# A diffusion step on one core: decay products issued a step ahead, prompt experts shared between two engines, and an earlier last slot

## The reference

```python
for l in range(DEPTH):                                   # 2 layers
    yp, ... = trunk_layer(yp, cond_ctx, lp, None, None)  # prompt
    ys, _   = trunk_layer(ys, cond_lat, lp, rope, ...)   # sample, reads the context caches

def trunk_layer(x, cond, lp, rope, ctx):
    m = silu(cond) @ lp['w_ada'] + lp['b_ada']
    sh1, sc1, g1, sh2, sc2, g2 = jnp.split(m, 6, axis=-1)
    mix, ctx_out = mixer(rmsnorm(x, n1) * (1 + sc1) + sh1, ...)
    x = x + g1 * mix
    x = x + g2 * peer_ffn(rmsnorm(x, n2) * (1 + sc2) + sh2, ...)

# mixer: x @ w_in -> attention | SSD scan, forward and backward | conv module -> concat @ w_out
# SSD of one chunk of 128 tokens and one direction, 8 heads:
lmat   = jnp.exp(segsum(a))                              # decays between tokens
scores = jnp.einsum('bclhn,bcshn->bhcls', ch, bh) * lmat
y_diag = jnp.einsum('bhcls,bcshp->bclhp', scores, xdt)
y_off  = ch . state . exp(a_cum)                         # then the state is updated

# peer_ffn, per block of 128 tokens: 8 heads choose 16 experts each, so 128 slots
s   = einsum(h @ w_q, sub_keys);  idx, gate = two-level top-16 of s
act = gelu(einsum('thkd,td->thk', u_tab[idx], hb))
out = einsum('thk,thkd->td', gate * act, v_tab[idx])
```

## Time and profile before

| | us |
|---|---|
| median of 3 runs | 4883.53 (4875.92 to 4887.87) |
| the profiled execution's own time | 4890.8 |
| its span in the trace | 4888.7 |
| PE / DVE / ACT / POOL busy | 3740.6 / 3316.4 / 876.5 / 1708.5 |
| granted TensorE clock, mean | 0.917 of full |

### The profile page before, as it was taken

How to read it: one execution, slowest core, us unless ns; L and a number is a source line. 1 busy time by engine, 2 the same in 40 slices (tenths; PEclk the granted TensorE clock), 3 DMA queues, 4 the chain that set the end, 5 groups by cost and what they waited for, 6 DMA issues and landing times.

```text
span 4888.7 us, 35992 instructions
## 1 busy us (share of the span) xinstructions
PE 3740.6 (77%) x10702; PEld 1857.5 (38%) x10702; DVE 3316.4 (68%) x8175; ACT 876.5 (18%) x2387; POOL 1708.5 (35%) x1374
## 2 busy tenths in 40 slices
PE   7578677858777778788878786785977787777776
PEld 6463434623232223235535443344432332322222
DVE  1546766666887868754574866666678887786666
ACT  0111125441101010010121111353310100100101
POOL 0001121573444435422222011217544454444432
PEclk9788788979999999999989897887999999999999
DMA  8335346775999999999969353557489999999998
GB/s 267 104 118 181 140 181 211 263 250 202 407 420 409 420 419 413 421 374 392 358 245 349 106 205 132 199 197 275 172 335 417 415 415 421 414 421 421 401 421 342
DMA packets 342147, 1497.68 MB, mean 306 GB/s; under 512 B 31424, under 2 KB 176448, under 8 KB 178112
## 3 DMA queue, kind: packets, MB, share of 16 engines
q0 software_dynamic: 184320, 1342.26, 68.8%
q1 hardware_dynamic: 157632, 153.13, 9.8%
HBM read 1491.97 MB, written 3.31 MB: 306 GB/s over the span
## 4 chain that ended last, share of the span: by engine, by line
PE 31%; DMA 30%; DVE 24%; POOL 5%; issue 5%; ACT 4%; SPq 1%; DVEq 0%; POOLq 0%; ACTq 0%
DMA uv_ring<-uv,expert_index 23%; PE expert_acc L766 13%; DVE uv_ring L1341 5%; DMA arena<-uv,expert_index 5%; PE rotating L997 4%; POOL arena L696 3%; PE rotating L795 3%; PE rotating L829 2%; DVE diag L1350 2%; POOL uv_ring L718 2%; DVE arena L1341 2%; DVE arena L1498 1%; DMA w_ring<-w_ada 1%; DVE arena L1711 1%; PE rotating L746 1%
## 5 line engine op out<-in xcount | busy, mean ns | idle before, releaser
L766 PE MATMUL expert_acc<-uv_ring,diag 128*128 128x512 f32 x3408 | 1723.8, 638 | 420.2 <-DVE diag L1350 410.2
L718 POOL DMA_INDIRECT uv_ring<-uv,expert_index x940 | 1103.3, 1174 | 2546.3 <-PE expert_acc L766 1994.4
L766 PEld LDWEIGHTS expert_acc<-uv_ring,diag 128*128 128x128 f32 x3408 | 626.8, 199 | 1407.5 <-DVE diag L1350 870.3
L1341 DVE CUSTOM_DVE_ANT_0 uv_ring<-uv_ring,arena 128x1024 f32<-128x1024 f32 x684 | 836.9, 1224 | 233.5 <-DMA uv_ring<-uv,expert_index 230.6
L766 PE MATMUL expert_acc<-arena,diag 128*128 128x512 f32 x1360 | 681.7, 628 | 179.4 <-DVE diag L1350 147.5
L1055 ACT ACTIVATE gelu<-u_dot 128x1 f32<-128x1 f32 x1280 | 260.2, 204 | 2868.8 <-DVE u_dot L1341 2868.1
L1350 DVE TENSOR_SCALAR diag<-const_mats,expert_gate,gelu 128x128 f32<-128x128 f32 x1192 | 437.2, 367 | 280.3 <-ACT gelu L1055 193.0
L718 POOL DMA_INDIRECT arena<-uv,expert_index x340 | 392.2, 1153 | 453.4 <-PE expert_acc L766 436.5
L1341 DVE CUSTOM_DVE_ANT_0 uv_ring<-uv_ring,prompt_rows 128x1024 f32<-128x1024 f32 x256 | 403.3, 1579 | 191.7 <-DMA uv_ring<-uv,expert_index 148.3
L1341 DVE CUSTOM_DVE_ANT_0 arena<-arena 128x1024 f32<-128x1024 f32 x340 | 416.1, 1224 | 92.9 <-DMA arena<-uv,expert_index 91.2
L766 PEld LDWEIGHTS expert_acc<-arena,diag 128*128 128x128 f32 x1360 | 240.3, 194 | 601.6 <-DVE diag L1350 380.6
(11 more groups left out here) (208 smaller groups left out, 3098.9 us busy)
## 6 DMA issues: line engine op xcount, KB each, us to landing
w_ring<-w_ada SPq DMA_DIRECT2D x66, 512.0 KB
w_ring<-w_in SPq DMA_DIRECT2D x64, 512.0 KB
w_ring<-w_pq SPq DMA_DIRECT2D x64, 512.0 KB
w_ring<-w_out SPq DMA_DIRECT2D x32, 512.0 KB
uv_ring<-w_ada SPq DMA_DIRECT2D x30, 512.0 KB, 5.5
uv_ring<-uv,expert_index POOLq DMA_INDIRECT x940
arena<-b_ada SPq DMA_DIRECT2D x48, 128.0 KB
arena<-uv,expert_index POOLq DMA_INDIRECT x340, 15.1
```

The costliest lines, as they stand in the source:

```text
L718: pool.indirect_dma_start(out=UV[j], out_offset=None, in_=uv, in_offset=bass.IndirectOffsetOnAxis(ap=idxs[:, n % 2, k:k + 1], axis=0)).the ...
L766: ins = pe.matmul(acc[:, half, :], diag[:, TURN[m] % DIAGS, :], UV[SLOT_AT[m]][:, D + 512 * half:D + 512 * half + 512], start=(k == 0), st ...
L1341: V_.tensor_tensor_reduce(UV[j][:, 0:D], UV[j][:, 0:D], rows_of(n), 1.0, 0.0, ALU.mult, ALU.add, dots[:, m % DOTS:m % DOTS + 1]).then_inc( ...
```

## The change

Three things are edited.

1. In the SSD loop TensorE issues the two dd products of step i+1 between yo and y of step i; only those of step 0 stand ahead of the loop. `psum_order` follows. On ACT the three gelus of a step's advances move behind the exponentials of the next step.
2. Among the prompt's slots, `by_pool` gave POOL all from 84 to 127 (44 of a layer). Now POOL has the odd ones from 84 to 107 and all from 108 on (32); the 12 even ones from 84 to 106 go to TensorE.
3. The table has 5 advances at n2 and 4 at pq tile 7, 145 in all. Slot 127, the fold and `add_peer` now stand at pq tile 7.

```diff
-                       ("head", range(24), 1), ("wo", range(0, 16, 2), 2), ("wo", range(1, 16, 2), 1), ("n2", [7], 3), ("pq", range(8), 2))
+                       ("head", range(24), 1), ("wo", range(0, 16, 2), 2), ("wo", range(1, 16, 2), 1), ("n2", [7], 5), ("pq", range(7), 2), ("pq", [7], 4))
...
-POOL_FROM = 84
+POOL_FROM, POOL_ALL = 84, 108
...
-    return n % NBLK == 0 and k >= POOL_FROM
+    return n % NBLK == 0 and (k >= POOL_FROM and k % 2 == 1 or k >= POOL_ALL)
...
-                    for i, (d, b) in enumerate(ssd_steps(g)):
+                    def decays(i):
+
                         pe.wait_ge(*s_arow.at(l, g, i))
                         for k in range(2):
                             t = fill("dd", l, g, 2 * i + k)
-                            done(pe.matmul(t, C[:, C_US if d else C_LS, :], Em[i % 2][:, 4 * k:4 * k + 4, :],
+                            done(pe.matmul(t, C[:, C_US if ssd_steps(g)[i][0] else C_LS, :], Em[i % 2][:, 4 * k:4 * k + 4, :],
                                            start=True, stop=True), "dd")
+
+                    decays(0)
+                    for i, (d, b) in enumerate(ssd_steps(g)):
...
                         done(pe.matmul(t, BC[:, 1, b * P:(b + 1) * P], Sbd[:, d, :], start=True, stop=True), "yo")
+                        if i + 1 < 2 * nb:
+                            decays(i + 1)
                         pe.wait_ge(*s_xdt.at(l, g, i))
...
                                                  ACT.Exp).then_inc(free["dd"].sem, 1)
-                        beside.point("st", i)
+                        if i:
+                            beside.point("st", i - 1)
+                    beside.point("st", 2 * nb - 1)
```

More of the change, by code:

```diff
@@ L289, in psum_order @@
             out += [("cT", l, g, b) for b in range(nb)]
+            out += [("dd", l, g, 0), ("dd", l, g, 1)]
             for i in range(2 * nb):
-                out += [("dd", l, g, 2 * i), ("dd", l, g, 2 * i + 1), ("yo", l, g, i), ("y", l, g, i), ("st", l, g, i)]
+                out.append(("yo", l, g, i))
+                if i + 1 < 2 * nb:
+                    out += [("dd", l, g, 2 * i + 2), ("dd", l, g, 2 * i + 3)]
+                out += [("y", l, g, i), ("st", l, g, i)]
             out += [("yT", l, g, b) for b in range(nb)]
```

## The result

The changed kernel takes 4820.18 us (median of 4 runs, 4817.62 to 4825.25) beside 4885.7 us for the kernel before, run on the same chip (4 runs, 4875.92 to 4891.81): a ratio of 0.9869, 95% interval 0.985 to 0.9888. It is about 65 us faster. The profiled execution's span went from 4888.7 to 4819.6 us.

What follows compares the result with a forecast made beforehand. No engine being full in SSD, it read chains: DVE's there, POOL's cycle in the output stage, POOL then TensorE in the query projection. SSD -46, output stage -6, query projection +21.6 gave -30, from 4883.5 to 4853 us; range 4825 to 4886.

Steps and rivals of the forecast that it cites:

- Exponential waits, -41.8: SSD: DVE's waits for exponentials go except in step 0; 20.0 us saved per sample, 3.83 in layer 1's prompt, 2 lost in layer 0's.
- The clock adds to it ... I take 4 in all, between 0 and 9: SSD samples: without the 2.7 us gap before y, y runs more often at TensorE's upper clock; 4 us saved in all.
- a wait at the upper clock is about 1.09: SSD: DVE's shortest wait for y, from the longest wait 2.4 less the 1.32 between two y rows; 2.8 us a sample.
- Output stage, -6: Output stage: POOL no longer longest, TensorE's tiles and sums plus waits set the time; 3 us saved a layer, 6 in all.
- The four waits: Output stage: TensorE waits for late-built diagonals at tiles 2, 6, 10 and 14, 3 us each, 12 together.
- Query projection, +21.6: Query projection: fold delays the second half 20.0 us, tail shrinks 9.2; net 10.8 us lost a layer, 21.6 in all.
- hold: Query projection: the fold, ahead of the transposes, waits for POOL's last add; second half starts 20.0 us later a layer.
- tail: End of query projection to the sample's first dot: 14.9 us before, forecast to get 9.2 us shorter a layer.
- The wait did not move to y: Rival, SSD: dd at the lower clock delays y, 46 saved becomes about 17; net 0, 4883 us; chance 0.13.
- TensorE's clock did not fall in the output stage: Rival, output stage: four waits drop TensorE's clock; at 0.70 the stage takes 126 us, total 4911; chance 0.09 for slower.
- rival of more from SSD and the output stage: SSD and output stage: every y at the upper clock (9 us), 8 a layer in output stage; 4840 us; chance 0.14.
- rival without a hold: Query projection: fold finds POOL done, so 18 us saved there; -70 in all, 4813 us; chance 0.10.

## Why the prediction missed

**Exponential waits, -41.8: right for the samples and layer 1's prompt.** 20.0 us a sample and 3.8 in that prompt went, as worked out. Layer 0's prompt lost 1.7 us of the 2 taken, but only 0.3 of them by the mechanism named, the pair ahead of the first y. The rest was the clock behind a gap of 3.73 us, so the near number is luck.

**"The clock adds to it ... I take 4 in all, between 0 and 9": this is the step that failed.** The same term measured 26 us in the samples' waits (y 5.5 + 7.4, st 6.7 + 6.8) and 3.9 more in layer 1's prompt, less the 1.4 lost in layer 0's. That is some 25 of the 35 us by which the forecast fell short. Two things were wrong in it. I took the y of 2.33 us for one at the upper clock, "a wait at the upper clock is about 1.09"; it was already touched by the fall, and the real values are 1.97 and 0.73. The 1.97 stood in my own rows: it is the first row, the same 16 matmul records, there behind a gap of 0.83 us. And I priced only y, though the text said that DVE stands three times in each step: st stands right behind y, took 2.02 us against 1.08 in 13 of the 16 steps, and its 8 us a sample were a row of the same view as the earlier trace rows. The mechanism was named and the direction right; the term was over six times too small, and its upper bound, built from y alone, too low as well. The two experiments on the gap, one filling it in the old order and one opening it in the new, show it from both sides.

The Trainium skill, "TensorE: Matmul & The Clock Gate", section "Why this matters for your kernels", says that idle gaps between bursts put the clock back to half. The traces agree that the clock falls around such gaps, but not that each gap brings it to half for the product behind it: of the 14 y products behind a gap of 2.96 us, four took 3.65 us and three 1.97. The prediction took the rule for every y as 10.6 us a sample and set it aside; y's part was 5.5 and 7.4 us, so that was right for y. With st's part, which it did not price, it is 12.2 us in layer 0 and 14.2 in layer 1.

**Output stage, -6: near, in part by luck.** 9.1 us were measured up to the first query tile, but 3.1 us of each layer's 4.6 and 4.5 lie in the norm behind the stage, which the sum did not have. From the first tile to the end of the last dot it is 98.8 us against 100.3, so 1.5 saved a layer, half of the 3 taken. The four waits are there, at 2.4 to 2.6 us instead of 3, with four small ones beside them: 11.7 us in all, for the 12 taken. The granted clock was 0.95, not 0.92. Left out were the drain of the last tile and the dot behind it, 2.0 us.

**Query projection, +21.6: right.** +17.8 measured, hold 36.4 of 40, tail -18.6 of -18.4. TensorE stood 23.13 us before the fold ("some 24"), and 5.8 us lie between the end of the last query matmul and the sample's first dot (1142.0 to 1147.76). The forecast had "about 6" and called it the time from the last score, though its sum counts from the last query matmul.

**The rivals.** None decided. The wait did not move to y, POOL was not done at the fold, and TensorE's clock did not fall in the output stage (0.95). The rival of more from SSD and the output stage, 0.14, has the right place but was sized by the same wrong bound, 9 us for the clock. The time of 4820 lies nearest to the 4813 of the rival without a hold, which the trace rules out: TensorE stood 23.13 us before the fold.

## What to carry to other kernels

When a gap ahead of a matmul is removed, price every product behind it up to the engine's next stand at both clocks, and take the upper-clock duration from a stretch whose granted clock is 1.00, not from a row of a stretch at 0.85. To test whether a gap costs clock, fill it with a repeat of the product before it: if the kernel gets faster by added work, the gap did cost. An item that waits for a slow engine belongs late in a queue, where its input has long arrived: the same fold cost 17 to 19 us a layer ahead of the transposes and under 2 us four tiles into the second half.

## What the runs showed of the hardware

At a gap of 3.08 us y itself could still run in 1.97 us, and only st and the sums behind it were slow (1.70, and 3.00 where 1.88 is usual); gaps of 1.76 us in each step left the granted clock at 1.00 in six steps in a row. One of them:

```profile
632.50:645.30 12.80, 10.87 (x36) 5.41 (x37) 11.72 (x23) 4.25 (x8) 4.34 (x3) 1.00 0.69 245
```

So the fall can show in the matmuls behind the one that ended the gap, and not in that one.

One small operation of DVE's in the norm took 2.94 us in the kernel before (2.93 in layer 1), where its like take 0.17, while POOL ran a gather and an add of 2.35 us; with the split, without adds there, it takes 0.17:

```profile
1010.90 2.35 POOL L696 TENSOR_TENSOR arena<-uv_ring,arena 128x1024 f32<-128x1024 f32 x1
1013.52 0.95 POOL L718 DMA_INDIRECT uv_ring<-uv,expert_index  x1 [0.27 <-POOL arena L696]
1014.49 2.35 POOL L696 TENSOR_TENSOR arena<-uv_ring,arena 128x1024 f32<-128x1024 f32 x1
```

```profile
1013.94 2.94 DVE L1314 TENSOR_SCALAR newton<-newton 128x4 f32<-128x4 f32 x1
```

The operation ends with the add, at 1016.9; this is most of the 3.1 us that the norm got shorter with the split. The Trainium skill, "SBUF — State Buffer", section "SBUF: two separate sides", has DVE and GpSimd share a pair of ports: a DVE operation in a two-port mode, or with two inputs in SBUF, and one of GpSimd's lock each other out for a whole instruction. The common end is in keeping with it. But the trace does not show the mode of this one-input operation, its row begins 0.55 us before the add's, and no run here varied the two alone, so the cause is not shown.

POOL's gathers show something like it, and they are part of its pace of 4.30 us a slot. Between 906 and 1115 us of the kernel before, 35 gathers were issued while DVE ran a dot, and they took 1.3 to 1.8 us; the seven others took 0.95. In the changed kernel, 880 to 1085 us, it was 12 of 15 beside a dot, and none of the 26 others. The gather of the earlier trace rows, 1.65 us from 940.81 on, stands beside this dot, which itself took 3.29 us instead of 1.22:

```profile
938.34 3.29 DVE L1341 CUSTOM_DVE_ANT_0 uv_ring<-uv_ring,prompt_rows 128x1024 f32<-128x1024 f32 x1 [0.21 <-DMA uv_ring<-uv,expert_index]
```

So of the 4.30 us some 0.7 come only with a dot that DVE runs at the same time. Which of the two holds the other up, and how, no run tests.
